# Retention of a two-layer decoder trunk: head products grouped by kind, and row loads moved ahead

## What is computed

```python
def retention(q, k, v):                      # each (b, 8 heads, 1024, 64), 8 chunks of 128
    ...
    scores = jnp.einsum('bhcid,bhcjd->bhcij', q_c, k_c) * decay[None, :, None]
    y_intra = jnp.einsum('bhcij,bhcje->bhcie', scores, v_c)
    chunk_kv = jnp.einsum('bhcjd,bhcje->cbhde', k_c * k_decay, v_c)
    def step(state, kv):
        return chunk_decay * state + kv, state
    _, prev_states = lax.scan(step, jnp.zeros(...), chunk_kv)
    y_inter = jnp.einsum('bhcid,cbhde->bhcie', q_c * q_decay, prev_states)
    return (y_intra + y_inter).reshape(b, h, s, d)
```

## Time and profile before

| | |
|---|---|
| median of 3 runs | 2167.11 us (2167.07 to 2169.96) |
| profiled execution | 2173.11 us |
| its span in the trace | 2171.4 us |
| mean granted TensorE clock in it | 0.908 of 2.4 GHz |
| PE busy | 1873.8 us, 86% of the span |
| PE weight load busy | 1548.8 us |
| VectorE busy | 1223.7 us |
| ScalarE busy | 865.5 us |

### The profile page before, as it was taken

How to read it: one execution, slowest core, us unless ns; L and a number is a source line. 1 busy time by engine, 2 the same in 40 slices (tenths; PEclk the granted TensorE clock), 3 DMA queues, 4 the chain that set the end, 5 groups by cost and what they waited for, 6 DMA issues and landing times. The chain is left out here.

```text
span 2171.4 us, 25604 instructions
## 1 busy us (share of the span) xinstructions
PE 1873.8 (86%) x9608; PEld 1548.8 (71%) x9608; DVE 1223.7 (56%) x1566; ACT 865.5 (40%) x928; POOL 317.4 (15%) x258
## 2 busy tenths in 40 slices
PE   8999999655789999986999992799999959999980
PEld 7888888645577788865888772688887847888760
DVE  5223322366555544565999883633324557999873
ACT  4111221231233333234888882311112126888860
POOL 0000000000110000111443420000000112434420
PEclk9999889685799999987999996899999978999995
DMA  5333212340200003455999966521124348999947
GB/s 199 127 117 107 99 57 78 117 95 1 78 1 1 1 1 104 167 190 230 362 381 372 367 269 224 173 58 50 39 65 164 135 178 325 381 381 372 373 161 296
DMA packets 145297, 374.40 MB, mean 172 GB/s; under 512 B 40078, under 2 KB 75150, under 8 KB 120446
## 3 DMA queue, kind: packets, MB, share of 16 engines
q1 hardware_dynamic: 113542, 309.54, 38.9%
q0 software_dynamic: 22432, 45.53, 5.8%
q10 hardware_dynamic: 9216, 17.93, 2.2%
HBM read 331.38 MB, written 75.10 MB: 187 GB/s over the span
## 5 line engine op out<-in xcount | busy, mean ns | idle before, releaser
L1242 PE MATMUL ex_ps_h<-even_split 128*128 128x512 f32 x768 | 195.9, 406 | 9.2 <-DVE even_split L1356 9.0
L1242 PE MATMUL ex_ps_h<-odd_split 128*128 128x512 f32 x768 | 196.0, 406 | 8.9 <-DVE odd_split L1356 8.5
L511 PE MATMUL in_ps<-in_w_hi,in_xT_hi 128*128 128x512 f32 (+1 forms) x448 | 179.1, 400 | 1.7 <-DVE in_xT_lo L416 1.7
L1242 PEld LDWEIGHTS ex_ps_h<-even_split 128*128 128x128 f32 x768 | 142.5, 192 | 48.7 <-DVE even_split L1356 14.9
L1242 PEld LDWEIGHTS ex_ps_h<-odd_split 128*128 128x128 f32 x768 | 142.5, 192 | 48.4 <-DVE odd_split L1356 15.3
L511 PE MATMUL in_ps<-in_w_lo,in_xT_hi 128*128 128x512 f32 (+1 forms) x448 | 175.0, 391 | 0.0
L511 PE MATMUL in_ps<-in_w_hi,in_xT_lo 128*128 128x512 f32 (+1 forms) x448 | 174.3, 389 | 0.0
L1630 PE MATMUL conv_ps<-conv_xT_hi,conv_w_hi 128*128 128x512 f32 x384 | 150.4, 392 | 0.9 <-DVE conv_w_lo L1568 0.9
L1630 PE MATMUL conv_ps<-conv_xT_lo,conv_w_hi 128*128 128x512 f32 x384 | 149.8, 390 | 0.0
L1630 PE MATMUL conv_ps<-conv_xT_hi,conv_w_lo 128*128 128x512 f32 x384 | 149.7, 390 | 0.0
L2333 ACT ACTIVATE att_prob<-att_ps_s 128x512 f32<-128x512 f32 x114 | 67.9, 597 | 175.3 <-PE att_ps_s L2271 175.1
(11 more groups left out here) (343 smaller groups left out, 4060.9 us busy)
## 6 DMA issues: line engine op xcount, KB each, us to landing
all_region<-in_moe_w_gate SPq DMA_DIRECT2D x16, 1024.0 KB
all_region<-in_moe_w_up SPq DMA_DIRECT2D x16, 1024.0 KB
all_region<-in_moe_w_down SPq DMA_DIRECT2D x16, 1024.0 KB
experts_w_gu<-in_moe_w_gate SPq DMA_DIRECT2D x16, 1024.0 KB
experts_w_gu<-in_moe_w_up SPq DMA_DIRECT2D x16, 1024.0 KB
experts_w_d<-in_moe_w_down SPq DMA_DIRECT2D x16, 1024.0 KB, 15.0
all_region<-in_ev_w_in SPq DMA_DIRECT2D x12, 1024.0 KB, 7.5
proj<-in_stage ACTq DMA_DIRECT2D x48, 256.0 KB, 2.0
```

Of the source, the lines that this page charges most:

```text
L511: last = pe.matmul(ps[:, q % BANKS, 0:n], a[:, k, at], w_part[:, b % 2, k, 0:n], start=(k == 0 and j == 0), stop=(k == KT - 1 and j == 2))
L1242: last = pe.matmul(ps_h[:, u % 2, :], a[:, u % 2, k, :], w[:, k, :], start=(k == 0 and j == 0), stop=(k == KT - 1 and j == 2))
```

## The change

In `score` and `weigh` the loops run "for b: for a:", so that neighbouring matmuls use different partition halves. In `weigh` the 8 matmuls with the values come first and the 8 with the states after them; the first matmul into each of the two PSUM banks opens it, the last closes it. The loads of the heads' queries move out of `rows_of_heads` to the end of SP's queue in `project_and_retain`: they wait until the last block of weights is split (the place is free) and until the tile's queries are in memory. And all 8 tiles of the stream's rows are loaded at the end of `experts`, none in `mix_and_conv` and `finish`.

```diff
@@ project_and_retain, SP
                     for c in range(2):
                         load_weights(b, c)
+                for c in range(2):
+                    sp.wait_ge(lo_ready[c], n_blocks)
+                for t in range(NT):
+                    in_memory(sp, QUERIES, t)
+                    ahead.load_queries(sp, t)
@@ score(c)
-                    for a in range(2):
-                        at = slice(a * HD, (a + 1) * HD)
-                        for b in range(PAIRS):
+                    for b in range(PAIRS):
+                        for a in range(2):
+                            at = slice(a * HD, (a + 1) * HD)
                             last = pe.matmul(ps_s[:, a, b, :], qkT[at, 1, b, :], qkT[at, 0, b, :], start=True, stop=True)
...
-                    for a in range(2):
-                        for b in range(PAIRS):
+                    for b in range(PAIRS):
+                        for a in range(2):
                             h = 2 * b + a
                             last = pe.matmul(ps_kv[a * HD:(a + 1) * HD, b, :], kd[:, h * HD:(h + 1) * HD],
@@ weigh(c)
-                    for a in range(2):
-                        at = slice(a * HD, (a + 1) * HD)
-                        for b in range(PAIRS):
+                    for b in range(PAIRS):
+                        for a in range(2):
                             h = 2 * b + a
                             pe.matmul(ps_y[:, a, b * HD:(b + 1) * HD], scores[:, a, b, :],
-                                      qkv[...], start=True, stop=False)
+                                      qkv[...], start=(b == 0), stop=False, skip_group_check=True)
+                    for b in range(PAIRS):
+                        for a in range(2):
+                            at = slice(a * HD, (a + 1) * HD)
                             last = pe.matmul(ps_y[:, a, b * HD:(b + 1) * HD], qdT[at, b, :], state[at, b, :],
-                                             start=False, stop=True)
+                                             start=False, stop=(b == PAIRS - 1), skip_group_check=True)
@@ NextRows, experts, mix_and_conv, finish
-    def load(self, sp, tiles):
-        for t in tiles:
+    def load(self, sp):
+        for t in range(NT):
...
-                following.load(sp, range(NT // 2))
+                following.load(sp)
...
-                ahead_rows.load(sp, range(NT // 2, NT))
...
-                    if t >= NT // 2:
-                        ahead_rows.load(sp, [t])
@@ new class, made before the projection; rows_of_heads takes it and drops its own load_queries
+class HeadRows:
+    def __init__(self, m, proj, region):
+        self.proj, self.loaded = proj, m.sems("head_rows_loaded", NT)
+        self.nq, self.kv, self.kvc = region.head_rows()
+    def load_queries(self, sp, t):
+        sp.dma_start(self.nq[:, t, :], self.proj[t * P:(t + 1) * P, C_NQ:C_KC]).then_inc(self.loaded[t], 16)
```

More of the change, by code:

```diff
@@ L188, in load, with project_and_retain @@
             sp.dma_start(self.raw[b][:, at, :], self.w_k[:, at, b * COLS:(b + 1) * COLS]).then_inc(self.loaded[2 * b + c], 16)
-def project_and_retain(nc, name, src, gain, w, width, out, ret_gain, con, y_out, cst, region):
+def project_and_retain(nc, name, src, gain, w, width, out, ret_gain, con, y_out, cst, region, ahead):
     n_blocks = -(-width // COLS)
@@ L199, in project_and_retain @@
     PAIRS = RH // 2
-    VALUES, GATE = 2, 3
+    VALUES, GATE, QUERIES = 2, 3, 4
     with Pool_(nc, name) as m:
@@ L543, in weigh @@
                     pe.wait_ge(decayed, c + 1)
-                    for a in range(2):
-                        at = slice(a * HD, (a + 1) * HD)
-                        for b in range(PAIRS):
+                    for b in range(PAIRS):
+                        for a in range(2):
                             h = 2 * b + a
                             pe.matmul(ps_y[:, a, b * HD:(b + 1) * HD], scores[:, a, b, :],
-                                      qkv[:, c % 2, 2 * RET_W + h * HD:2 * RET_W + (h + 1) * HD], start=True, stop=False)
+                                      qkv[:, c % 2, 2 * RET_W + h * HD:2 * RET_W + (h + 1) * HD],
+                                      start=(b == 0), stop=False, skip_group_check=True)
+                    for b in range(PAIRS):
+                        for a in range(2):
+                            at = slice(a * HD, (a + 1) * HD)
                             last = pe.matmul(ps_y[:, a, b * HD:(b + 1) * HD], qdT[at, b, :], state[at, b, :],
-                                             start=False, stop=True)
+                                             start=False, stop=(b == PAIRS - 1), skip_group_check=True)
                     last.then_inc(y_ready, 1)
@@ L1675, with rows_of_heads @@
 KEY_EXT = EXT + 2 * R
-def rows_of_heads(nc, name, proj, q_gain, k_gains, cst, con, keep, region):
+class HeadRows:
[4 more added lines that the diff above has]
+        sp.dma_start(self.nq[:, t, :], self.proj[t * P:(t + 1) * P, C_NQ:C_KC]).then_inc(self.loaded[t], 16)
+def rows_of_heads(nc, name, proj, q_gain, k_gains, cst, con, keep, ahead):
     NK = 2 * G
@@ L1683, in rows_of_heads @@
     with Pool_(nc, name) as m:
-        nq, kv, kvc = region.head_rows()
+        nq, kv, kvc = ahead.nq, ahead.kv, ahead.kvc
         gains = m.sb("gains", [P, 3, HD])
@@ L1693, in rows_of_heads @@
         ps_n = m.ps("ps_n", [P, 3, ROUND, P])
-        rows_loaded, keys_loaded, pool_loaded, rest_loaded, mask_loaded = (
-            m.sems("rows_loaded", NT), m.sem("keys_loaded"), m.sem("pool_loaded"), m.sem("rest_loaded"), m.sem("mask_loaded"))
+        rows_loaded = ahead.loaded
+        keys_loaded, pool_loaded, rest_loaded, mask_loaded = (
+            m.sem(n) for n in ("keys_loaded", "pool_loaded", "rest_loaded", "mask_loaded"))
         eps_ready, n_squared, n_summed, n_rooted, rows_added, n_ready = (
@@ L1703, in _ @@
             def _(sp):
-                def load_queries(t):
-                    sp.dma_start(nq[:, t, :], proj[t * P:(t + 1) * P, C_NQ:C_KC]).then_inc(rows_loaded[t], 16)
-                load_queries(0)
                 for j, (a, b) in enumerate(((C_KS, C_VS), (C_KW, C_VW))):
@@ L1712, in _ @@
                 sp.dma_start(q_rows[:], con["q_rows"].rearrange("p (t h j) -> p t h j", t=NT, h=NH)).then_inc(keys_loaded, 16)
-                for t in range(1, NT):
-                    load_queries(t)
                 for j, (a, b) in enumerate(((C_KC, C_VC), (C_VC, C_KS))):
@@ L2517, in route @@
                                   data, lists, rows)
+            head_rows = HeadRows(top, proj, region)
             with Pool_(nc, "in") as m:
                 project_and_retain(nc, "in0", a["x"][0, :, :], a["mix_norm_g"][0, :], a["ev_w_in"][0, :, :], IN_W, proj,
-                                   a["ev_ret_norm_g"][0, :], con, mixer, cst, region)
+                                   a["ev_ret_norm_g"][0, :], con, mixer, cst, region, head_rows)
             with Pool_(nc, "even") as held:
@@ L2531, in trunk @@
                             rows_of_heads(nc, "heads", proj, a["ev_q_norm_g"][0, :], a["ev_k_norm_g"][0, :, :], cst, con, keep,
-                                          region)
+                                          head_rows)
                             sparse_prepare(nc, "prep", a["ev_q_norm_g"][0, :], a["ev_k_norm_g"][0, :, :], a["ev_cmp_pe"][0, :, :, :],
```

## The result

The changed kernel took 2115.11 us (median of 4 runs, 2112.67 to 2118.32), the kernel before on the same chip 2168.45 us (4 runs, 2167.07 to 2169.96): ratio 0.9755, 95% interval 0.9737 to 0.9773, so 49 to 57 us less. In a later comparison with 5 runs it took 2113.94 against 2172.57 us, ratio 0.973 (0.971 to 0.9751), 58.6 us less. Forecast were 2106.5 us, 2097 to 2124. The profiled execution after took 2113.19 us (span 2111.5, mean clock 0.919) against 2173.11 before: 59.9 us between the two profiles, against a sum of 60.6.

The account below looks back on a forecast made before the run. PE was taken as the bound, busy 86% of the span. Savings of 28.3 + 25.5 + 1.5 + 2.0 + 3.3 = 60.6 us gave 2112.5 us profiled and 2106.5 for the median, range 2097 to 2124.

Parts of the forecast that it names:

- The projection: Retention chunks in the projection: 28.3 us from shorter weighing and score, plus 25.5 us from the clock's return.
- Weighing: Each chunk's weighing at full clock: 3.0 us instead of 5.7, saving 2.7 us a chunk.
- no fall left: Weighings and products behind them: clock stays 1.00 instead of dropping to half speed; 25.5 us, bounds 0 and 27.
- rows 5: Profile rows of the score, where partition halves ran side by side; taken as model for the states, 0.9 us.
- the clock does not come back: Rival for the projection's chunks: half-speed stretches stay in every weighing, time 2132 us; chance 0.08.
- 4.5 us for its clock: Last chunk of the projection: 10.1 us of low clock instead of 6.8, so 4.5 us gained instead of 3.0.
- The prediction's sentence on the score: Score: a promised up to 2x would save 0.8 of its unpacked 1.6 us, but half is had already.
- term of 0.55 us: Queries times keys in the score: with all records overlapping, the last starts at 0.9 instead of 1.44 us.
- The queries: Query loads moved out of the heads' stage: its first rows land sooner, 1.5 us gained, bounds 0.4 and 2.7.
- ScalarE's and VectorE's loop, which keeps its length: Heads' stage after its first rows land: the loop there was taken as unchanged in length by the moved loads.
- The rows: Stream rows loaded after the last expert: net 2.0 us in the convolution and 3.3 us at the end.
- The scatter's delay: Last scatter of each experts' stage, delayed by added row loads: 2.0 us each time, bounds 0 and 4.

Follow-up runs that it names:

- The parts alone: The kernel before with only the weighing reordered, 2126.21 us, ratio 0.9798; and with only the score's two loops alternating partition halves, 2159.31 us, ratio 0.995.
- weigh_alone: The kernel before with only the weighing reordered, values first, then states alternating between partition halves: 2126.21 against 2171.81 us, ratio 0.9798.
- grouped_by_pair: The kernel before with the weighing grouped by pairs of heads, two matmuls with values, then two with states, four times over: 2146.18 us, run once.
- queries_alone: The kernel before with only the heads' query loads moved to the end of the projection's queue: 2166.77 us (12 runs), ratio 0.9985.
- the filler: The kernel before with eight extra 256-column matmuls, results unread, in the middle of each interleaved weighing: 2167.04 us, run once, beside 2172.11.

## Why the prediction was right, and where its terms were off

**The projection, 53.8 us forecast, 53.0 in the profiles.** Weighing 3.0 us forecast (2.86 from its start to the product's), score's group 1.2 (1.16), period 27.7 (27.60), last copy near 361 (360.80), no fall left: each step as put. The parts alone give 44 and 11 us. Choosing rows 5 for the states was right (1.11 us), and the rival *the clock does not come back* is refuted by weigh_alone and by the windows. The Trainium skill, TensorE: Matmul & The Clock Gate, section Part 1: The HAM clock gate, ties the half clock to idle windows; grouped_by_pair has the fall with PE at 34.00 of 34.00 us, so here the measurement speaks against that as the only cause, as far as the profile's busy time can tell. The Trainium skill, TensorEngine Tiling (Array Packing), section Key Properties, says that changing the tiling mode drains the engine; the trace agrees, with 0.147 us a change.

One step of it was too coarse, though the error is small. The last chunk was given 4.5 us for its clock, as if the product behind the last weighing ended the stage in the changed kernel too. Two stores end it, POOL's of the last weighing's normalised rows and ScalarE's of the last product. Before:

```profile
414.12 0.55 POOL L314 DMA_DIRECT2D mixer<-in_y  x1 [24.62 <-DVE in_y L456]
...
415.65 0.33 ACTq L344 DMA_DIRECT2D proj<-in_stage  x1
```

POOL's lands after 2.7 us, at 416.8, and ScalarE's after 1.8, at 417.4; the next stage starts 0.6 us later, at 418.00. So before, the product was on the path. After:

```profile
361.18 0.55 POOL L320 DMA_DIRECT2D mixer<-in_y  x1 [17.49 <-DVE in_y L462]
361.28 0.33 ACTq L350 DMA_DIRECT2D proj<-in_stage  x1
```

ScalarE's lands after 2.6 us, at 363.9, POOL's after 3.3, at 364.5, and the stage starts 0.5 us after that. Now the normalising and its store are what is waited for. That is why the last copy came 54.4 us earlier and the stage only 53.0: 1.4 us of the gain were lost when the path changed over.

The prediction's sentence on the score calls 1.6 us unpacked; these are the 1.64 us measured with half the overlap, and by its own 0.112 us a record 16 records unpacked take 1.79. Its term of 0.55 us does not rest on that.

**The queries, 1.5 us forecast.** The size was about right (3.3, 0.7 to 5.9, alone), the place wrong. ScalarE begins 9.48 us after the stage's first issue (364.99 to 374.47) instead of 9.78 (forecast 8.3): 0.3 us, below the lower bound of 0.4. The issue of `q_rows` comes 0.5 us sooner after the stage's first (2.76 instead of 3.29), but it lands after 6.6 us instead of 6.4: the DMA engines stay at 0.93 of their time over the stage's first 10 us (0.91 before), so other loads seem to have taken the place of the queries. "ScalarE's and VectorE's loop, which keeps its length" is the step that failed. PE's first matmuls of the tiles, before and after:

```profile
435.74 1.10 PE L1839 MATMUL heads_ps_n<-all_ident,heads_qa 128*81 128x128 f32 x8 [0.47 <-DVE mix_qT L1811]
...
442.48 1.99 PE L1839 MATMUL heads_ps_n<-all_ident,heads_qa 128*81 128x128 f32 x8 [5.21 <-DVE mix_qT L1811]
```
```profile
383.81 1.10 PE L1855 MATMUL heads_ps_n<-all_ident,heads_qa 128*81 128x128 f32 x8 [1.85 <-DVE mix_qT L1827]
...
387.24 1.10 PE L1855 MATMUL heads_ps_n<-all_ident,heads_qa 128*81 128x128 f32 x8 [1.89 <-DVE mix_qT L1827]
```

From the first tile to the last it is 27.3 us before and 24.1 after. In the seven kernels that load the queries in the stage it is 27.2 to 28.5, in the six that load them ahead 24.1 to 26.7, with no overlap. In the first rhythm the tiles come in pairs, 3.2 us and then mostly 4.9 or more, and in the first two pairs of before VectorE waits 1.5 and 1.6 us for ScalarE's squares; in the profile after one tile follows the other every 3.4 us. That the loads' place decides is shown by these thirteen, queries_alone above all; through what, is not.

**The rows, 5.3 us forecast (2.0 and 3.3).** The gains came as put: 4.6 us in the convolution's stretch (3.95), 5.9 in `finish` (5.3). The scatter's delay was the mis-sized term: 3.6 and 3.7 us where 2.0 each was taken, close to the upper bound of 4 (and the first is 4.4 beside the 8.5 us usual in the other kernels). Net 3.2 us in the profiles (4.6 + 5.9 - 3.6 - 3.7), 0 alone, 3 in the whole change, both uncertain by as much. The middle of a range was no argument, since the delay could be estimated: eight transfers of 512 KB need 11.0 us at 0.38 MB/us, the scatter is issued 7.0 us after the first of them (1257.87 to 1264.91), and 4.0 us of them still stand ahead of it. The traces bear out the mechanism, and the size less exactly: about the last scatter the loads' last packets end 6.7 us after its issue, where they ended 1.0 us after it before, and its own last packet ends at 2069.5, just behind theirs at 2069.3.

**From the sum to the median.** The near match of the sum with the profiles is in part luck: the queries' stretch gave 3.7 us instead of 1.5, the rows 3.2 instead of 5.3, and the two errors cancel. The sum matched the profiles (60.6 against 59.9) and the repeated comparison (58.6), but not the first (53.3, 49 to 57). The forecast lay 8.6 us low: 6.0 because the saving, read from an execution of 2173.1 us, was taken off the median of 2167.11; 0.7 because the profiled execution after took 2113.19 instead of 2112.5; 1.9 because the median after lies that much above its own profiled execution. Later runs gave medians of 2171.81 (23 runs) and 2172.57 (9 runs) for the kernel before, so its profiled execution was an ordinary one and the median of three a low base. Both are within the spread of this kernel's executions.

## What to carry to other kernels

Look at the granted clock even where PE is 100% busy: here a few microseconds of thin matmuls whose contraction alternates cost 2.7 us in themselves and some 3 us more by the clock, most of it in the product behind them. Put matmuls of one contraction size together and let neighbours of 64 partitions alternate halves; each change avoided was 0.147 us here. And a load moved into an idle gap lies over whatever ends that gap: price the delay of that transfer at what is left of the load that stands ahead of it, and look whether the wait comes back elsewhere when it is moved once more.

## What was not expected of the hardware

The clock fell in some chunks and not in others with the same instructions (5 of 8 in grouped_by_pair, 3 of 8 with the filler), and low stretches lasted 3.4, 6.8 or 10.2 us. A stage's next step on POOL took 2.6 us with idle DMA engines and 4.6 or 5.4 us while 512 KB transfers streamed, although that step moves none of that data. The halves of the array overlap in part even when the program issues all of one half first: 1.60 us for 16 records, against 1.11 alternating and an estimated 1.8 with no overlap (16 x 0.112).
